# Per-layer tokens transposed and split among the last 24 down products, state rows turned in a bank of their own

## The chip, the cores and the metric

The kernel runs on one core of one Trainium2 chip. A core has five engines that run side by side: TensorE (PE in the profile; its weight loads are PEld), VectorE (DVE), ScalarE (ACT), GpSimd (POOL) and SyncE (SP). They meet through semaphores: an instruction adds to one when it ends, and another engine's queue stands still until the count is reached. Each engine works through its own queue strictly in order, so a wait holds up everything behind it on that engine. Products are written to PSUM, eight banks of 128 x 512 fp32 numbers. The metric is device time in microseconds.

## What is computed

One inference step of a two-layer encoder on 1024 prompt tokens and 64 sample tokens. Each layer is attention, a gated feed-forward part with a short convolution (ConvFFN), and a gated per-layer embedding. The change lies at the joint of the last two:

```python
def conv_ffn(h, w_in, conv_w, conv_b, w_out, pad):
    u = h @ w_in
    up = jnp.concatenate([pad, u], axis=1)
    c = conv_b + sum(up[:, j:j + T] * conv_w[j] for j in range(3))
    g, val = jnp.split(c, 2, axis=-1)
    y = (jax.nn.silu(g) * val) @ w_out
    return y, up[:, -2:]            # the state rows

def ple(x, p, g_norm, w_gate, w_proj):
    gate = jax.nn.sigmoid(rmsnorm(x, g_norm) @ w_gate)
    return (p @ w_proj) * gate      # p: 256 numbers per token and layer

x = x + conv_ffn(rmsnorm(x, ffn_norm[i]), ...)
x = x + ple(x, p[i], ...)
```

All numbers are fp32. The model's width is 1024, the feed-forward part's 2816.

## The kernel before

The residual `x` lies in SBUF with the 1024 channels in eight planes of 128 partitions and the 1088 tokens along the free dimension. Tokens are worked on in three segments (`SEGS`) of 384, 384 and 320. Every product is made from three: both operands are split into a high part (rounded) and a low part (the rest), and high x high, high x low and low x high are added up in PSUM; the three matmuls are lines L1164 to L1166. Weights come in chunks of 1024 columns; SyncE loads a chunk, ScalarE or GpSimd rounds it, and GpSimd makes the low part (L899 the rounding, L905 the rest).

**The down products.** The product with `w_out` is made in six steps `down(j)` of 24 jobs each, a job being one plane of `x` and one segment. Steps 0 to 4 take four tiles of the hidden width, the last (j = 5) only two, with six matmuls per job. A job writes one PSUM bank; VectorE adds it to `x` and counts `add_done`. In the last step the banks are `LAST_BANKS` (7, 4, 6, 5, 3), so banks 0, 1 and 2 stand free once the step before has been added. VectorE's `add_rows` (adds on L2405) also adds up planes of squares for the next norm (`squares_between`, L2415), the squares being made by ScalarE (`square`, L1782; the last plane per segment in `square_last`, L1793).

**Behind the last job**, in this order:

- TensorE turns the convolution's state rows (`tail`, two transposes on L1630) into banks 0 and 1; VectorE copies them out (L2839), ScalarE issues their stores (L2216).
- TensorE waits for the loaded per-layer tokens (`ptok`), for the copies of the state rows and for all adds, and makes 18 transposes (L1643) into banks 0 to 5.
- ScalarE rounds the six results (L2220), VectorE makes the six low parts (L2845), counted by `p_low`.
- TensorE waits for all six, and makes the norm's mean (`norm`, L1212 and L1213). ScalarE loads its table (L1799) and makes the reciprocal root (`root`, L1804, L1806), and VectorE normalises; meanwhile TensorE runs the 24 jobs of `p @ w_proj` (`row_jobs`), which ScalarE copies out between its other steps (`pj`).

The tokens are loaded by ScalarE's queue (L2208, 1 MB, and L2209, 64 KB) at the start of its `ple`. Ahead of them in that queue stands the rounding of the last weight chunk of the feed-forward part (`weights_high`, L1819), which waits until all chunks of steps 0 to 4 have been used.

Of the kernel before, what the change touches and what calls it, by code (L numbers as in the profile page):

```python
# [19 lines left out]
F32 = mybir.dt.float32  # L20
F32R = mybir.dt.float32r
ALU = mybir.AluOpType
ACT = mybir.ActivationFunctionType
AX = mybir.AxisListType

P = 128
D = 1024
KT = D // P
# [21 lines left out]
F_ADDS = 6  # L50
# [165 lines left out]
def program(nc, x_prompt, x_sample, p_prompt, p_sample, cache_a_k, cache_a_v, cache_b_k, cache_b_v,  # L216
# [6 lines left out]
    with ctx:  # L223
# [937 lines left out]
        def _(pe):  # L1161
# [357 lines left out]
            def ffn(l):  # L1519
# [67 lines left out]
                def down(j):  # L1587

                    b, tiles, wide = j % 2, 4 if j < 5 else 2, 2 if j < 5 else 4
                    for job in range(24):  # L1590
# [28 lines left out]
                        m.then_inc(gemm_done if r < 3 * wide - 1 else chunk_done, 1)  # L1619

# [7 lines left out]
                pe.wait_ge(u_kept, U_KEPT * (l + 1))  # L1628
                for kind in range(2):
                    pe.transpose(ps[0:88, kind, 0:P], tail[:, 88 * kind:88 * kind + 88], ident[:, :]).then_inc(tail_turned, 1)  # L1630

            def ple(l):
                c0 = at[f"P{l}"][0]
                nn = 2 if l == 0 else 5
                pe.wait_ge(p_loaded, 32 * (l + 1))
                pe.wait_ge(tail_kept, 2 * (l + 1))
                pe.wait_ge(add_done, ADDS[f"F{l}"] + 24 * F_ADDS)
                for k in range(2):
                    for s in range(3):
                        j = 3 * k + s  # L1640
                        for b in range(3):
                            rows = P if 3 * s + b < 8 else TS
                            m = pe.transpose(ps[:, j, 128 * b:128 * b + rows], ptok[0:rows, 3 * s + b, 128 * k:128 * k + 128],  # L1643
                                             ident[0:rows, 0:rows])
                        m.then_inc(p_turned, 1)
# [123 lines left out]
        def _(act):  # L1769
# [25 lines left out]
            def root(n, s):  # L1795

                a, w = SEGS[s]
                if s == 0:
                    act.preload_act_table_set("natural_log_exp_and_others")  # L1799
# [404 lines left out]
            def ple(l, n):  # L2204
                c0, g0 = at[f"P{l}"]
                act.wait_ge(chunk_done, c0 - 2)
# [3 lines left out]
                squares(n, add_done, ADDS[f"F{l}"] + 24 * (F_ADDS - 1), 3)  # L2210
                act.wait_ge(add_done, ADDS[f"F{l}"] + 24 * F_ADDS)
                for s in range(3):
                    square_last(n, s)
                for r, dram in enumerate((conv_p, conv_s)):
                    act.wait_ge(tail_kept, 2 * l + r + 1)
                    act.dma_start(dram[l, 0].rearrange("r (n p) -> (r n) p", p=P), tail_rows[:, r, :]).then_inc(conv_stored, 16)  # L2216
                for k in range(2):
                    for s, (a, w) in enumerate(SEGS):
                        act.wait_ge(p_turned, 6 * l + 3 * k + s + 1)
                        act.activation(act_hi[:, k, a:a + w], ps[:, 3 * k + s, 0:w], ACT.Copy).then_inc(p_high, 1)  # L2220
                act.wait_ge(conv_stored, 32 * (l + 1))
                for s in range(3):
                    root(n, s)
                for j in range(24):
# [5 lines left out]
                    a, w = SEGS[j % 3]  # L2230
# [822 lines left out]
```

## Time and profile before

| | |
|---|---|
| median of 3 runs | 3120.36 us (3115.38 to 3126.84) |
| the profiled execution | 3117.31 us, its span 3115.5 us |
| TensorE busy | 2965.0 us, 95% of the span |
| weight loads | 2858.6 us |
| VectorE busy | 2089.9 us, 67% |
| ScalarE busy | 1327.9 us, 43% |
| GpSimd busy | 1528.1 us, 49% |
| DMA | 234.23 MB, mean 75 GB/s |

The profile follows one execution on the chip. A timeline row gives the start in microseconds from the start of the span, the duration, the engine, the line of the kernel, the operation with output and input, and how often it stands in a row; brackets at the end hold the idle time before it and what ended it. An engine's name with a q (ACTq) is its queue issuing a DMA. The chain of waits is followed back from the last instruction of the program, at each step to what released it. PEclk is the clock that TensorE was granted: 1.00 is 2.4 GHz, 0.50 is 1.2 GHz.

### The profile page before, as it was taken

The page shows a single profiled execution, that of the slowest core. Times are in us where ns is not written, and L with a number is a line of the kernel's source. Part 1 is how long each engine was busy: PE and PEld are TensorE (multiplying, and loading weights), DVE is VectorE, ACT ScalarE, POOL GpSimd, SP SyncE. Part 2 cuts the span into 40 slices and gives each one's busy share as a digit, 9 for nine tenths or more (in the row PEclk, how much of TensorE's full clock was granted, in tenths as well). Part 3 has the DMA queues.
Part 4 walks back from the last instruction along what each step waited for, and adds up shares of the span by engine and source line. Part 5 has one row for each costly group of instructions (what it writes and reads, how often), then busy time and mean ns, then how long its engine had stood idle before and what let it go on. Part 6 is the DMA issues. An engine that isn't in the chain of part 4 may idle for free.

```text
span 3115.5 us, 47514 instructions
## 1 busy us (share of the span) xinstructions
PE 2965.0 (95%) x18469; PEld 2858.6 (92%) x18469; DVE 2089.9 (67%) x3171; ACT 1327.9 (43%) x2692; POOL 1528.1 (49%) x975
## 2 busy tenths in 40 slices
PE   7999999898999999999989999999899999999998
PEld 6888888798999999999978888889899999999997
DVE  6666666528888888334676777772888888833475
ACT  4555555315444443112432666651544444311243
POOL 2222122234788884212335778763488888421231
PEclk8999999899999999999989999999999999999999
DMA  5232222411222224211105121131122222421111
GB/s 118 61 72 71 75 64 69 135 42 48 77 76 79 71 77 165 98 62 57 41 15 148 31 61 53 55 129 41 55 73 74 79 70 79 162 103 58 58 39 64
DMA packets 282190, 234.23 MB, mean 75 GB/s; under 512 B 29860, under 2 KB 264052, under 8 KB 281972
## 3 DMA queue, kind: packets, MB, share of 16 engines
q1 hardware_dynamic: 267160, 217.29, 23.4%
q10 hardware_dynamic: 14812, 13.97, 1.4%
q8 instruction: 145, 2.38, 0.3%
q14 instruction: 73, 0.60, 0.1%
HBM read 168.63 MB, written 62.58 MB: 74 GB/s over the span
## 4 chain that ended last, share of the span: by engine, by line
PE 76%; DVE 14%; ACT 5%; issue 3%; POOL 1%; DMA 1%; ACTq 0%; SPq 0%; DVEq 0%; POOLq 0%
PE ps L1164 22%; PE ps L1166 21%; PE ps L1165 21%; PE ps L1347 2%; PE ps L1482 2%; ACT t L1932 2%; PE ps L1300 2%; PE ps L1283 2%; DVE t L2452 2%; PE ps L1367 2%; DVE t L2431 2%; DVE t L2602 1%; DVE t L2525 1%; ACT t L1988 1%; DVE ps L2517 1%
## 5 line engine op out<-in xcount | busy, mean ns | idle before, releaser
L1164 PE MATMUL ps<-t,t 128*128 128x384 f32 (+1 forms) x4760 | 1591.0, 334 | 48.6 <-ACT t L2106 10.4
L1166 PE MATMUL ps<-t,t 128*128 128x384 f32 (+1 forms) x4760 | 1560.9, 328 | 0.0
L1165 PE MATMUL ps<-t,t 128*128 128x384 f32 (+1 forms) x4760 | 1559.7, 328 | 0.0
L1164 PEld LDWEIGHTS ps<-t,t 128*128 128x128 f32 x4760 | 898.9, 189 | 80.3 <-issue 33.7
L1165 PEld LDWEIGHTS ps<-t,t 128*128 128x128 f32 x4760 | 900.1, 189 | 1.2 <-issue 0.5
L1166 PEld LDWEIGHTS ps<-t,t 128*128 128x128 f32 x4760 | 899.3, 189 | 0.0
L947 POOL TENSOR_TENSOR t<-t,t 128x512 fp32r<-128x512 f32 x280 | 473.6, 1710 | 31.8 <-ACT t L2057 22.1
L905 POOL TENSOR_TENSOR t<-t,t 128x1024 fp32r<-128x1024 f32 x101 | 250.4, 2479 | 435.0 <-ACT t L1819 431.6
L2802 DVE TENSOR_TENSOR t<-t,ps 128x384 f32<-128x384 f32 (+1 forms) x240 | 126.2, 531 | 274.0 <-PE ps L1166 274.0
L2731 DVE SCALAR_TENSOR_TENSOR t<-t,t,t 128x1090 f32<-128x1090 f32 x88 | 192.9, 2192 | 91.4 <-ACT t L2053 90.3
L2057 ACT ACTIVATE t<-t 128x512 fp32r<-128x512 f32 x320 | 193.1, 625 | 130.6 <-POOL t L955 50.8
L899 POOL TENSOR_TENSOR t<-t,t 128x1024 fp32r<-128x1024 f32 x51 | 104.1, 2040 | 262.1 <-PE ps L1166 261.6
L1819 ACT ACTIVATE t<-t 128x1024 fp32r<-128x1024 f32 x50 | 53.0, 1060 | 374.1 <-PE ps L1166 374.1
L1117 POOL TENSOR_TENSOR t<-t,t 128x128 f32<-128x128 f32 (+5 forms) x144 | 162.2, 1147 | 100.0 <-DVE t L2969 98.4
L2053 ACT ACTIVATE t<-t,t 128x1090 f32<-128x1090 f32 x88 | 114.7, 1304 | 224.4 <-DVE t L2716 224.4
L2733 DVE SCALAR_TENSOR_TENSOR t<-t,t,t 128x1090 f32<-128x1090 f32 x88 | 190.0, 2159 | 3.1
L2602 DVE TENSOR_TENSOR t<-ps,t 128x512 fp32r<-128x512 f32 (+1 forms) x184 | 115.6, 632 | 68.6 <-ACT t L1988 66.1
L1932 ACT ACTIVATE t<-ps,t 128x128 f32<-128x128 f32 (+5 forms) x144 | 105.6, 737 | 92.6 <-DVE t L2525 92.6
L1988 ACT ACTIVATE t<-ps 128x512 fp32r<-128x512 f32 (+1 forms) x184 | 101.2, 550 | 94.3 <-PE ps L1283 90.9
L1015 POOL TENSOR_TENSOR t<-t,t 128x384 fp32r<-128x384 f32 (+1 forms) x24 | 23.2, 966 | 225.5 <-ACT t L1956 225.5
L1482 PE MATMUL ps<-t,t 128*128 128x256 f32 (+1 forms) x656 | 118.9, 298 | 13.9 <-DVE t L2628 6.3
L955 POOL TENSOR_TENSOR t<-t,t 128x512 f32<-128x512 f32 x40 | 79.4, 1984 | 91.8 <-DMA t<-in_w_ffn_in 48.0
(191 smaller groups left out, 4071.1 us busy)
## 6 DMA issues: line engine op xcount, KB each, us to landing
t<-in_w_ffn_in SPq DMA_DIRECT2D x160, 256.0 KB, 2.9
ff_dram<-t SPq DMA_DIRECT2D x44, 544.0 KB
t<-ff_dram SPq DMA_DIRECT2D x44, 544.0 KB, 6.1
t<-in_w_ffn_out SPq DMA_DIRECT2D x44, 512.0 KB, 3.4
t<-in_w_qkv_a SPq DMA_DIRECT2D x24, 512.0 KB, 4.0
t<-in_w_ple_gate SPq DMA_DIRECT2D x16, 512.0 KB, 3.8
out<-t SPq DMA_DIRECT2D x32, 192.0 KB, 2.1
t<-in_w_o_a SPq DMA_DIRECT2D x8, 512.0 KB, 4.1
```

The costliest lines, as they stand in the source:

```text
L905: pool.tensor_tensor(w_lo[slot][:, :], w_raw[slot][:, :], w_hi[slot][:, :].bitcast(F32), ALU.subtract).then_inc(w_split, 1)
L947: pool.tensor_tensor(lo, raw, hi.bitcast(F32), ALU.subtract).then_inc(blk_split, 1)
L1117: pool.tensor_tensor(probs, probs, rz[:, c + m:c + m + 1].broadcast_to([P, w]), ALU.mult).then_inc(scaled, 1)
L1164: pe.matmul(out, a_hi, b_hi, start=start, stop=False, skip_group_check=True)
L1165: pe.matmul(out, a_hi, b_lo, start=False, stop=False, skip_group_check=True)
L1166: return pe.matmul(out, a_lo, b_hi, start=False, stop=stop, skip_group_check=True)
L1482: mm = pe.matmul(ps[:, 6, 0:256], v_both[r:P, vi, :], part[r:P, k % 2, 256 * b:256 * b + 256], start=g == 0 and b == 0 and part is bT_hi, ...
L1932: act.activation(p_a[n % 2][:, m, 0:w], psf[:, 1024 * m:1024 * m + w], ACT.Exp, bias=negmax[:, col:col + 1], accum_out=zsum[:, col:col + 1 ...
L2057: act.activation(S[name][0], S[name][2], ACT.Copy).then_inc(blk_high, 1)
L2602: dve.tensor_tensor(bT_lo[:, k % 2, 0:w], ps[:, 4 + k % 2, 0:w], bT_hi[:, k % 2, 0:w].bitcast(F32), ALU.subtract).then_inc(t_free, 1)
L2731: dve.scalar_tensor_tensor(dst, ub[:, 1:T + 3], col(44), dst, ALU.mult, ALU.add).then_inc(conv_step, 1)
L2733: dve.scalar_tensor_tensor(dst, ub[:, 0:T + 2], col(0), dst, ALU.mult, ALU.add).then_inc(conv_step, 1)
```

## The change

The 18 transposes of the per-layer tokens move from behind the last 24 down jobs to among them: nine behind job 1 and nine behind job 7, both into banks 0 to 2. ScalarE rounds each group between its squares, VectorE makes the low parts behind its adds 4 and 10. The state rows are turned into one bank, 3, at two offsets. ScalarE loads the table of the root before it waits for the last adds, issues the stores of the state rows behind the roots, and waits for these stores only before it copies out job 12 of `p @ w_proj`. The wait for chunks ahead of the token loads goes out.

```diff
--- before.py
+++ after.py
@@ -1617,6 +1617,22 @@
                             m = three(ps[:, bank, 0:w], w_hi[c % 2][:, cc:cc + 128], w_lo[c % 2][:, cc:cc + 128],
                                       h_hi[:, 4 * b + k, a:a + w], h_lo[:, 4 * b + k, a:a + w], k == 0, k == tiles - 1)
                         m.then_inc(gemm_done if r < 3 * wide - 1 else chunk_done, 1)
+                        if j == 5 and job in (1, 7):
+                            turn_layer_tokens(job // 6)
+
+                def turn_layer_tokens(k):
+
+                    if k == 0:
+                        pe.wait_ge(p_loaded, 32 * (l + 1))
+                        pe.wait_ge(add_done, a0 + 112 + JOB_BANKS.index(0) + 1)
+                    else:
+                        pe.wait_ge(p_low, 6 * l + 3)
+                    for s in range(3):
+                        for b in range(3):
+                            rows = P if 3 * s + b < 8 else TS
+                            m = pe.transpose(ps[:, s, 128 * b:128 * b + rows], ptok[0:rows, 3 * s + b, 128 * k:128 * k + 128],
+                                             ident[0:rows, 0:rows])
+                        m.then_inc(p_turned, 1)
 
                 first_up(c0)
                 for n in range(PAIRS):
@@ -1626,23 +1642,15 @@
 
                 pe.wait_ge(tail_set, 2 * NU * (l + 1))
                 pe.wait_ge(u_kept, U_KEPT * (l + 1))
+                pe.wait_ge(add_done, a0 + 24 * F_ADDS - 4)
                 for kind in range(2):
-                    pe.transpose(ps[0:88, kind, 0:P], tail[:, 88 * kind:88 * kind + 88], ident[:, :]).then_inc(tail_turned, 1)
+                    pe.transpose(ps[0:88, 3, 128 * kind:128 * kind + 128], tail[:, 88 * kind:88 * kind + 88],
+                                 ident[:, :]).then_inc(tail_turned, 1)
 
             def ple(l):
                 c0 = at[f"P{l}"][0]
                 nn = 2 if l == 0 else 5
-                pe.wait_ge(p_loaded, 32 * (l + 1))
-                pe.wait_ge(tail_kept, 2 * (l + 1))
                 pe.wait_ge(add_done, ADDS[f"F{l}"] + 24 * F_ADDS)
-                for k in range(2):
-                    for s in range(3):
-                        j = 3 * k + s
-                        for b in range(3):
-                            rows = P if 3 * s + b < 8 else TS
-                            m = pe.transpose(ps[:, j, 128 * b:128 * b + rows], ptok[0:rows, 3 * s + b, 128 * k:128 * k + 128],
-                                             ident[0:rows, 0:rows])
-                        m.then_inc(p_turned, 1)
                 pe.wait_ge(p_low, 6 * (l + 1))
                 norm(nn)
                 row_jobs(c0, 0, 0, act_hi, act_lo, pj_kept, lambda k: 24 * l + k)
@@ -1792,10 +1800,10 @@
                 act.wait_ge(acc_done, 6 * (n - 1) + 5)
                 act.activation(sq[1][:, a:a + w], x[:, KT - 1, a:a + w], ACT.Square).then_inc(sq_last, 1)
 
-            def root(n, s):
+            def root(n, s, loaded=False):
 
                 a, w = SEGS[s]
-                if s == 0:
+                if s == 0 and not loaded:
                     act.preload_act_table_set("natural_log_exp_and_others")
                 if n:
                     act.wait_ge(mean_done, 3 * (n - 1) + s + 1)
@@ -2203,24 +2211,30 @@
 
             def ple(l, n):
                 c0, g0 = at[f"P{l}"]
-                act.wait_ge(chunk_done, c0 - 2)
                 act.wait_ge(ff_low, NFF * (l + 1))
                 act.dma_start(ptok[:, 0:8, :], p_prompt[l, 0].rearrange("(b p) d -> p b d", p=P)).then_inc(p_loaded, 16)
                 act.dma_start(ptok[0:TS, 8, :], p_sample[l, 0]).then_inc(p_loaded, 16)
-                squares(n, add_done, ADDS[f"F{l}"] + 24 * (F_ADDS - 1), 3)
+
+                def layer_tokens_high(k):
+
+                    for s, (a, w) in enumerate(SEGS):
+                        act.wait_ge(p_turned, 6 * l + 3 * k + s + 1)
+                        act.activation(act_hi[:, k, a:a + w], ps[:, s, 0:w], ACT.Copy).then_inc(p_high, 1)
+
+                for k in range(KT - 1):
+                    if k in (1, 3):
+                        layer_tokens_high(k // 2)
+                    act.wait_ge(add_done, ADDS[f"F{l}"] + 24 * (F_ADDS - 1) + 3 * (k + 1))
+                    square(n, k)
+                act.preload_act_table_set("natural_log_exp_and_others")
                 act.wait_ge(add_done, ADDS[f"F{l}"] + 24 * F_ADDS)
                 for s in range(3):
                     square_last(n, s)
+                for s in range(3):
+                    root(n, s, True)
                 for r, dram in enumerate((conv_p, conv_s)):
                     act.wait_ge(tail_kept, 2 * l + r + 1)
                     act.dma_start(dram[l, 0].rearrange("r (n p) -> (r n) p", p=P), tail_rows[:, r, :]).then_inc(conv_stored, 16)
-                for k in range(2):
-                    for s, (a, w) in enumerate(SEGS):
-                        act.wait_ge(p_turned, 6 * l + 3 * k + s + 1)
-                        act.activation(act_hi[:, k, a:a + w], ps[:, 3 * k + s, 0:w], ACT.Copy).then_inc(p_high, 1)
-                act.wait_ge(conv_stored, 32 * (l + 1))
-                for s in range(3):
-                    root(n, s)
                 for j in range(24):
                     half = j // 12
                     if j % 12 < 11:
@@ -2228,6 +2242,8 @@
                     else:
                         act.wait_ge(chunk_done, c0 + half + 1)
                     a, w = SEGS[j % 3]
+                    if j == 12:
+                        act.wait_ge(conv_stored, 32 * (l + 1))
                     act.activation(pj[:, j // 3, a:a + w], ps[:, 4 + j % 4, 0:w], ACT.Copy).then_inc(pj_kept, 1)
                     high_step(n, j)
 
@@ -2833,17 +2849,27 @@
                 add_tiles(0, range(4, 24))
                 for j in range(1, 5):
                     add_tiles(j)
-                add_rows(c0 + 24, g0 + 108, 0, 0, 0, squares_between(2 + 3 * l, 22), LAST_BANKS)
+
+                def layer_tokens_low(k):
+
+                    for s, (a, w) in enumerate(SEGS):
+                        dve.wait_ge(p_high, 6 * l + 3 * k + s + 1)
+                        dve.tensor_tensor(act_lo[:, k, a:a + w], ps[:, s, 0:w], act_hi[:, k, a:a + w].bitcast(F32),
+                                          ALU.subtract).then_inc(p_low, 1)
+
+                add_squared = squares_between(2 + 3 * l, 22)
+
+                def between(job):
+                    add_squared(job)
+                    if job in (4, 10):
+                        layer_tokens_low(job // 6)
+
+                add_rows(c0 + 24, g0 + 108, 0, 0, 0, between, LAST_BANKS)
+                dve.wait_ge(tail_turned, 2 * l + 2)
                 for kind in range(2):
-                    dve.wait_ge(tail_turned, 2 * l + kind + 1)
-                    dve.tensor_copy(tail_rows[:, kind, :], ps[0:88, kind, 0:P]).then_inc(tail_kept, 1)
+                    dve.tensor_copy(tail_rows[:, kind, :], ps[0:88, 3, 128 * kind:128 * kind + 128]).then_inc(tail_kept, 1)
             def ple(l, n):
                 c0, g0 = at[f"P{l}"]
-                for k in range(2):
-                    for s, (a, w) in enumerate(SEGS):
-                        dve.wait_ge(p_high, 6 * l + 3 * k + s + 1)
-                        dve.tensor_tensor(act_lo[:, k, a:a + w], ps[:, 3 * k + s, 0:w],
-                                          act_hi[:, k, a:a + w].bitcast(F32), ALU.subtract).then_inc(p_low, 1)
                 normalise(n)
                 dve.wait_ge(pj_kept, 24 * (l + 1))
                 st = n
```

## Rows read from the trace of the kernel before

**Rows 1.** Page of the profile, chain that ended last: shares by engine.

```profile
PE 76%; DVE 14%; ACT 5%; issue 3%; POOL 1%; DMA 1%; ACTq 0%; SPq 0%; DVEq 0%; POOLq 0%
```

**Rows 2.** Timeline of TensorE, first of the last 24 products: start, us, instruction.

```profile
1449.93 0.34 PE L1164 MATMUL ps<-t,t 128*128 128x384 f32 x1
...
1452.04 0.31 PE L1164 MATMUL ps<-t,t 128*128 128x320 f32 x1
...
1452.91 0.34 PE L1164 MATMUL ps<-t,t 128*128 128x384 f32 x1
```

**Rows 3.** Timeline of ScalarE, same stretch, with its DMA issues.

```profile
1450.27 0.37 ACTq L2208 DMA_DIRECT2D t<-in_p_prompt  x1
1450.68 0.61 ACTq L2209 DMA_DIRECT2D t<-in_p_sample  x1
```

**Rows 4.** Chain of waits, end of layer 0's down products: start, us, what.

```profile
1470.91 1.29 DVE t L2415
...
1472.63 1.12 ACT t L1782
1473.78 1.29 DVE t L2415
...
1475.51 0.52 ACT t L1793
...
1476.81 0.39 ACT t L2220
1477.22 2.76 DVE t L2845 x6
1480.02 0.91 PE ps L1212 x2
1480.93 0.65 PE ps L1213 x2
```

**Rows 5.** Timeline of TensorE, behind layer 0's down products.

```profile
1475.97 2.50 PE L1643 MATMUL ps<-t,t 128*128 128x128 f32 x18 [1.82 <-DVE t L2839]
```

**Rows 6.** Lines L2208, L2209 (issue to landing) and L2216 (ns of an issue).

```profile
DMA to landing us min/median/max: 5.4/5.4/5.4
...
DMA to landing us min/median/max: 5.5/5.6/5.7
...
L2216 ACTq DMA_DIRECT2D out<-t x4: 325/348/580, 1475.7 to 2954.6; - x4
```

**Rows 7.** Timelines of ScalarE and TensorE, the same place in layer 1.

```profile
2929.24 0.62 ACTq L2209 DMA_DIRECT2D t<-in_p_sample  x1
...
2930.59 0.31 PE L1164 MATMUL ps<-t,t 128*128 128x320 f32 x1
```

**Rows 8.** Timelines of GpSimd and VectorE, weight passes beside vector work.

```profile
1474.02 2.81 POOL L899 TENSOR_TENSOR t<-t,t 128x1024 fp32r<-128x1024 f32 x1 [5.83 <-PE ps L1166]
...
1498.41 2.60 POOL L905 TENSOR_TENSOR t<-t,t 128x1024 fp32r<-128x1024 f32 x1
...
1498.67 2.75 DVE L2431 TENSOR_TENSOR t<-t,t 128x384 fp32r<-128x384 f32 x1
```

**Rows 9.** Windows: length, busy PE, PEld, DVE, ACT, POOL, PEclk, DMA share.

```profile
754.00:759.00 5.00, 0.72 (x5) 0.46 (x4) 4.96 (x4) 0.00 (x0) 2.55 (x3) 1.00 0.37 123
...
760.00:762.00 2.00, 2.00 (x7) 2.00 (x8) 1.58 (x4) 2.00 (x5) 1.23 (x1) 0.50 0.01 4
...
763.00:765.00 2.00, 2.00 (x14) 2.00 (x13) 1.97 (x2) 1.51 (x3) 1.29 (x1) 1.00 0.00 0
...
1476.00:1478.50 2.50, 2.46 (x18) 1.92 (x18) 1.28 (x3) 2.50 (x8) 2.42 (x2) 1.00 0.14 36
...
1612.80:1623.00 10.20, 7.64 (x19) 5.66 (x19) 7.46 (x10) 8.39 (x12) 3.12 (x2) 0.50 0.00 0
```

**Rows 10.** Timeline of TensorE, the next norm's mean; idle before it in brackets.

```profile
1602.62 1.65 PE L1212 MATMUL ps<-t,t 128*128 128x384 f32 x2 [2.16 <-DVE t L2415]
1604.06 1.49 PE L1213 MATMUL ps<-t,t 128*128 128x384 f32 x2
```

## Prediction, made before the changed kernel was run

> **What bounds the kernel now.** I first read the page's chain of work that ended last: the matrix engine holds three quarters of it and the vector engine a seventh [rows 1]. A change of a few microseconds has to be judged in its own stretch, so I then read the timelines around the last 24 down products and the start of the per-layer embedding, once per layer.
>
> In the last 24 products TensorE runs without a break: one group of three jobs starts at 1449.93 and the next at 1452.91, so three jobs take 2.98 us, two wide and one narrow [rows 2]. Behind the products the chain of waits leaves TensorE [rows 4]. VectorE adds a plane of squares, then the last product; ScalarE squares the last plane (1475.51), rounds the transposed tokens (1476.81), VectorE makes their low halves (six in 2.76 us), and only then does the mean of the norm start, at 1480.02. TensorE's only work in that hole is the tail's two transposes and the eighteen token transposes, 2.50 us [rows 5]. From the start of the last square to the mean 4.51 us pass per layer; that is all the change can win.
>
> ScalarE issues the two token loads at 1450.27 and 1450.68 [rows 3], a third of a microsecond and more into the first of these 24 jobs. They land 5.4 and 5.5 to 5.7 us after issue [rows 6]. Before the change nobody needs them until 1475.97, so this lateness costs nothing. The new code moves the user to where the lateness shows.
>
> **The change part by part**, both layers together unless it says otherwise.
>
> *Removed from the chain (A).* The mean no longer waits for the roundings, the low halves and the transposes; it waits for the last product's sum and one square (0.52 us) [rows 4]. The table load moves ahead of that wait, where ScalarE has nothing else to do; it was hidden behind the low halves before. With a hand-over of some 0.03 us the mean starts 0.55 us after 1475.51 in place of 4.51. A = 2 x (0.55 - 4.51) = -7.9.
>
> *Added wait for the tokens (B).* The first nine transposes stand behind job 1 and wait for both loads. Job 1's last product has been issued by 1452.04 [rows 2]. The deleted wait for chunks on ScalarE wins no time: the same count is waited for by the weight rounding just ahead (`weights_high` of the last chunk), so the loads cannot be issued earlier. They are complete at 1450.68 + 5.7 = 1456.38; TensorE stands 4.34 us. In layer 1: 2929.24 + 5.5 = 2934.74 against 2930.59 [rows 7], 4.15 us. All products behind stand in order on TensorE, and so do the adds and squares that follow them. B = +8.5, between 7.2 (if the larger load alone counted, 3.63 us per layer) and 9.5 (half a microsecond of hand-over each). The other new wait there, for the add of the job that last used bank 0, is over long before: that job ended in the group before.
>
> *Transposes inside the products (C).* Eighteen at 2.50 us per layer [rows 5], now in a stream that TensorE sets: +5.0. They were on the chain before too; that part is already in A.
>
> *The second turn* waits for three low halves. Counted from the end of the first turn: job 2's sum, ScalarE's first square 1.12 us, three roundings at 0.39, three low halves at 0.46 [rows 4] put the third low half about 5.1 us later; six jobs take 2 x 2.98 = 5.96. It is hidden with 0.8 us to spare, at most 1.4 us per layer (three low halves) if not: taken as 0.
>
> *VectorE falls behind (D).* The three low halves of the second turn (1.4 us) stand behind add 10; some 0.3 us of it fits into VectorE's idle time, so 1.1 us of lag remain. Afterwards a plane of squares is added once per three jobs, each behind a square that waits for an add. Two such sums in the lagging state start at 1470.91 and 1473.78, 2.87 us apart [rows 4], against 2.98 us of three jobs [rows 2]: the lag shrinks by only 0.1 us a period, and some 0.8 us is left at the last add, three periods on. Beyond that, the last sum of squares now meets GpSimd. Before, it starts at 1473.78 and GpSimd's weight pass at 1474.02 [rows 4, 8]: VectorE is first by 0.24 us. With 0.8 us of lag it comes second, and where it comes second an operation on two SBUF operands takes 2.75 us while the weight pass runs [rows 8]; a low half of the same shape from PSUM takes 0.46 [rows 4]. I take half of about 1.4 us for this. D = 2 x (0.8 + 0.7) = +3.0, from 0 to 2 x (1.4 + 2.3) = 7.4.
>
> The Trainium skill (GPSIMD Engine Reference, section 8, Key points) has GpSimd share its SBUF interfaces with VectorE, against instructions with two SBUF inputs. By that rule the token low halves, which read PSUM, would run on undisturbed and the sums of squares would not; with the last sum blocked in full D would be 2 x (0.8 + 2.3) = +6.2 and the total below 17.4.
>
> *The clock behind the stall (E).* An idle of about five microseconds from 754.7 on is followed by 0.50 of the clock, that is 1.2 GHz, in 760 to 762, and by the full level after 763 [rows 9]. Some 3 us of products at half speed lose 1.5 us. I expect the same behind B: E = 2 x 1.5 = +3.0, from 0 to 3.4.
>
> *The clock at the mean (F).* In the old hole the eighteen transposes stand in the middle and the clock stays at 1.00 [rows 9]. Now the hole is one idle of 2.5 to 4 us. After one of 2.16 us the two pairs of the next norm's mean run from 1602.62 to 1605.55, 2.93 us [rows 10], against 0.91 + 0.65 = 1.56 here [rows 4]: 1.37 us per layer. I take 1.0: F = +2.0, from 0 to 3.4.
>
> The Trainium skill (TensorE: Matmul & The Clock Gate, Part 4: PE-mode transpose) says the full clock does not engage for transposes. By it the old hole should already have dropped, and moving the transposes would cost nothing, with F at 0 and the total at 12.2; the row shows 1.00 through the hole, and I go by the row.
>
> *Moved stores (G).* ScalarE now issues the two state stores between the roots and the first product copy. An issue takes 0.35 us in the median, at most 0.58 [rows 6]; the product copies have four banks in hand, so only the first normalised tile feels it. G = +0.6, from 0 to 1.8. The wait for these stores stands before copy 12 of 24, long after they have landed. The tail's transposes wait for add 19, which is done four jobs before; free.
>
> Sum: -7.9 + 8.5 + 5.0 + 3.0 + 3.0 + 2.0 + 0.6 = +14.2. The profiled execution took 3117.31, so 3131.5; the median of the runs is 3.05 higher, which gives 3134.6. I say 3133, +0.4%, just inside the half per cent (15.6 us) that a measurement of this kernel can about tell from no change.
>
> **The rivals.**
>
> *The tokens are there in time.* Then B and E vanish: 14.2 - 8.5 - 3.0 = +2.7, 3120.0 to 3123.1, and with D and F at their lower ends 7.9 - 5.0 - 0.6 = 2.3 us faster, 3115. It decides if the loads land within 1.4 us of the second issue. For it: a wait in ScalarE's queue ahead of the loads goes out. Against it: the landing of 5.4 to 5.7 us in both layers, and the issue still behind the same count. Chance 0.08.
>
> *The half clock lasts.* From 1612.8 to 1623.0 the clock stays at 0.50, with TensorE in short waits [rows 9]. If the products behind the stall run like that for 10 us, E is 2 x 5 = 10: total +21.2, 3138.5 to 3141.6, slower by 0.7%. It decides as soon as the half level lasts some 1.4 us longer per layer than my 3 us. For it: short waits do follow, for the second turn and the banks. Against it: behind the closest case in kind, a wait and then dense products, it lasted 3 us. Chance 0.10.
>
> *VectorE loses every meeting with GpSimd.* D = 7.4 in place of 3.0: +18.6, 3135.9 to 3139.0, slower by 0.6%. For it: the lead today is only 0.24 us. Against it: sums of squares in the middle of the stretch got through before. Chance 0.17.
>
> **How the numbers follow.** My forecast, stall with a sum of 8 to 18, has 0.65; of it about a fifth lies above 15.6. The lower ends give -7.9 + 7.2 + 5.0 = +4.3, the upper ends 22 to 23. So the range runs from 3119 to 3143. Slower by over 0.5%: 0.13 of my forecast, 0.10 and most of 0.17, 0.37. Faster by over 0.5% would need more than A itself: 0.02. The rest, 0.61, is within.
>
> **What would show it.** TensorE idle of 4 us behind job 1 of the last 24, ended by the token load; a granted clock of 0.50 for some 3 us behind it; the last product's sum of each layer some 8 to 10 us later than now, and the mean some 0.55 us after the last square begins. I am wrong if the load's landing is not what TensorE waits for, if the clock stays at 1.00 after the stall (then the total is nearer 9), or if the mean waits for something else, such as a table load at the roots.

## The result, and the profile after

The changed kernel takes 3137.66 us in the median of 4 runs (3137.37 to 3141.03), the kernel before, beside it, 3120.85 (3115.38 to 3126.84): ratio 1.0055, interval 1.0038 to 1.0072. On the medians it is 16.8 us slower; 3133 was forecast. The profiled execution took 3141.03 us, with a span of 3139.2. One execution of the wait-only kernel below took 4249.8 us at a granted clock of 0.63 and is left out of its median.

The timeline of TensorE of the changed kernel, layer 0 (start, length, line; idle before it in brackets), answers to [rows 2, 5]. L1633 are the token turns, L1647 the tail's turn, L1212 and L1213 the mean, L1164 a product.

```profile
1456.95 2.26 PE L1633 MATMUL ps<-t,t 128*128 128x128 f32 x9 [4.06 <-DMA t<-in_p_sample]
...
1459.14 0.63 PE L1164 MATMUL ps<-t,t 128*128 128x320 f32 x1
...
1466.70 1.24 PE L1633 MATMUL ps<-t,t 128*128 128x128 f32 x9
...
1483.76 0.38 PE L1647 MATMUL ps<-t,t 128*88 128x128 f32 x2
...
1488.14 1.62 PE L1212 MATMUL ps<-t,t 128*128 128x384 f32 x2 [4.00 <-ACT t L1801]
1489.55 1.49 PE L1213 MATMUL ps<-t,t 128*128 128x384 f32 x2
...
1494.14 0.58 PE L1164 MATMUL ps<-t,t 128*128 128x384 f32 x1
```

There are two holes of 4 us, one ended by the load of the sample's tokens, one by the last square. Behind each everything is slow: nine transposes take 2.26 us, while the second nine, with no wait, take 1.24. The windows of the same kernel (start:end, length, busy time of PE, PEld, DVE, ACT, POOL, granted clock, DMA share, GB/s) give the reason; they answer to [rows 9].

```profile
1455.00:1456.00 1.00, 0.00 (x0) 0.00 (x0) 0.00 (x0) 0.00 (x0) 0.00 (x0) 0.83 0.86 264
1456.00:1457.00 1.00, 0.05 (x1) 0.05 (x1) 0.00 (x0) 0.00 (x0) 0.00 (x0) 0.50 0.91 329
...
1461.00:1462.00 1.00, 1.00 (x5) 1.00 (x4) 0.49 (x1) 0.34 (x1) 0.00 (x0) 0.50 0.00 0
1462.00:1463.00 1.00, 1.00 (x6) 1.00 (x5) 0.12 (x1) 1.00 (x2) 0.00 (x0) 0.76 0.00 0
...
1487.00:1488.00 1.00, 0.00 (x0) 0.00 (x0) 0.84 (x4) 0.53 (x2) 1.00 (x1) 0.50 0.00 0
...
1492.00:1493.00 1.00, 1.00 (x3) 0.58 (x2) 0.75 (x2) 0.21 (x1) 0.00 (x0) 0.50 0.51 153
```

The clock falls to 0.50 (1.2 GHz) inside the stall and is back in 1462 to 1463: some 6.8 us at the half level. TensorE works in 5.5 of them, where the prediction had 3. At the mean the half level is as long, with TensorE working in 5.1 of it. The last view is the chain of waits of the changed kernel (it answers to [rows 4]) and, below it, GpSimd's timeline ([rows 8]).

```profile
1472.91 1.26 DVE t L2857 x3
...
1475.82 2.48 DVE t L2431
1478.30 0.41 DVE t L2421
...
1479.88 1.29 DVE t L2431
...
1485.62 1.43 DVE t L2431
...
1487.47 0.53 ACT t L1801
1488.01 0.14 issue
1488.14 1.62 PE ps L1212 x2
```

```profile
1474.75 2.41 POOL L905 TENSOR_TENSOR t<-t,t 128x1024 fp32r<-128x1024 f32 x1
```

The mean starts 0.67 us behind the first of the last squares, where it was 4.51: the part that was meant to win did so. But from 1471 on the chain no longer goes through TensorE, whose products are done at 1483.76. It goes through VectorE and ScalarE: through the three low halves of the second turn (L2857), then through the sum of squares at 1475.82, which begins while GpSimd's pass runs and takes 2.48 us. The page's shares by engine say less:

```profile
PE 68%; DVE 19%; ACT 7%; issue 4%; POOL 1%; DMA 1%; ACTq 0%; SPq 0%; DVEq 0%; POOLq 0%
```

TensorE has eight points less than in [rows 1], some 250 us, where the joint grew by 21. Most of that shift must be the chain taking another way elsewhere in the kernel; it was not traced.

### The profile page after: what moved, and what is told of

It is laid out like the page before. It is cut to its first block, busy times and chain, and to the rows that moved or that the text cites. A ratio compares the mean times of both kernels' runs of the same rounds, so it can differ in the third digit from the quotient of the medians.

```text
span 3139.2 us, 47516 instructions
## 1 busy us (share of the span) xinstructions
PE 2978.8 (95%) x18469; PEld 2870.0 (91%) x18469; DVE 2090.9 (67%) x3171; ACT 1329.3 (42%) x2692; POOL 1510.7 (48%) x975
## 4 chain that ended last, share of the span: by engine, by line
PE 68%; DVE 19%; ACT 7%; issue 4%; POOL 1%; DMA 1%; ACTq 0%; SPq 0%; DVEq 0%; POOLq 0%
PE ps L1164 19%; PE ps L1166 18%; PE ps L1165 18%; PE ps L1347 2%; DVE t L2747 2%; PE ps L1482 2%; ACT t L1940 2%; DVE t L2749 2%; PE ps L1300 2%; PE ps L1283 2%; PE ps L1367 2%; DVE t L2447 1%; DVE t L2468 1%; ACT t L2061 1%; DVE t L2618 1%
## 5 line engine op out<-in xcount | busy, mean ns | idle before, releaser
L1164 PE MATMUL ps<-t,t 128*128 128x384 f32 (+1 forms) x4760 | 1594.4, 335 | 49.5 <-ACT t L2114 10.4
L1164 PEld LDWEIGHTS ps<-t,t 128*128 128x128 f32 x4760 | 901.3, 189 | 80.5 <-issue 34.5
L947 POOL TENSOR_TENSOR t<-t,t 128x512 fp32r<-128x512 f32 x280 | 462.8, 1670 | 34.4 <-ACT t L2065 23.5
```

The costliest lines, as they stand in the source:

```text
L947: pool.tensor_tensor(lo, raw, hi.bitcast(F32), ALU.subtract).then_inc(blk_split, 1)
L1164: pe.matmul(out, a_hi, b_hi, start=start, stop=False, skip_group_check=True)
```

## The experiments

Each kernel below was timed beside the kernel before on the same chip. The table gives, for the profiled execution of each, the path through the joint in three pieces (layer 0 / layer 1, us): from the first of the last 24 products to the tail's turn; from there to the mean; from there to the first per-layer product copy on ScalarE. "Joint" is the sum over both layers less that of the kernel before (70.2); "median" is the difference of the medians.

```
kernel           to tail's turn  to mean      to first copy  joint   median  ratio [95%]
before           23.84 / 23.84   6.25 / 6.24  5.02 / 5.03
changed          33.15 / 33.51   4.38 / 4.38  8.00 / 8.00    +21.2   +16.8   1.0055 [1.0038, 1.0072]
changed, again   32.09 / 33.17   4.38 / 4.39  7.19 / 7.81    +18.8   +16.8   1.0061 [1.0048, 1.0075]
wait only        29.49 / 29.66   6.38 / 6.41  7.08 / 7.06    +15.9   +15.0   1.0043 [1.0029, 1.0057]
early load       26.43 / 26.41   4.38 / 4.38  7.20 / 8.21     +6.8    +5.9   1.0016 [1.0006, 1.0026]
turns in hole    32.08 / 33.87   4.38 / 4.39  5.50 / 5.28    +15.3   +18.1   1.0054 [1.0041, 1.0067]
early turns      26.42 / 26.41   2.40 / 2.40  7.19 / 6.97     +1.6    +2.2   1.0006 [0.9996, 1.0016]
early, filled    26.42 / 26.43   2.40 / 2.40  5.49 / 5.28     -1.8    -3.3   0.9990 [0.9981, 0.9999]
rows in hole     26.42 / 26.43   2.41 / 2.40  5.49 / 5.28     -1.8    -1.3   1.0000 [0.9991, 1.0009]
GpSimd later     26.40 / 26.40   3.07 / 3.06  5.49 / 5.35     -0.4    +4.4   1.0014 [1.0005, 1.0023]
stall filled     30.59 / 30.62   4.38 / 4.38  8.44 / 6.97    +15.2   +10.5   1.0035 [1.0023, 1.0047]
second in hole   25.14 / 25.14   2.41 / 2.40  5.49 / 5.28     -4.4    -5.0   0.9982 [0.9973, 0.9991]
stores later     25.14 / 25.15   2.39 / 2.40  4.98 / 4.98     -5.2    -1.4   0.9996 [0.9987, 1.0005]
products first   34.17 / 33.31   4.39 / 4.38  7.19 / 8.20    +21.4   +18.3   1.0063 [1.0046, 1.0079]
```

Single executions of one kernel differ by 10 us and more, so the two columns agree to a few microseconds at best. The kernels were timed in several groups, each beside the kernel before; where the text gives a difference of two medians of different groups, the one by the table stands beside it.

**The wait alone.** Before, and in its last 24 products:

```
                        m.then_inc(gemm_done if r < 3 * wide - 1 else chunk_done, 1)
+                       if j == 5 and job == 1:
+                           pe.wait_ge(p_loaded, 32 * (l + 1))
```

> The kernel before, with one line more: behind job 1 of the last 24 down products TensorE waits for the token loads of the layer. Nothing is moved; the transposes stay behind the products. Theory (the stall and the half clock behind it are what costs): TensorE stands about 4.1 us per layer behind job 1 and the six jobs behind it run some 2.7 us longer, so 2 x (4.1 + 2.7) = 13.6 us over the kernel before, about 3134. Rival (the stall is absorbed, since VectorE and ScalarE set the end of the stretch; what costs is the transposes and what stands behind them): 0 to 3 us over the kernel before, 3121 to 3124.

Measured +15.0: the wait by itself costs nearly as much as the whole change, with not one transpose moved. That the two are so close is partly chance, since this kernel has neither the change's gain (A of the prediction) nor its losses C, D and G. Its timeline of TensorE:

```profile
1455.13 0.63 PE L1164 MATMUL ps<-t,t 128*128 128x320 f32 x1 [3.95 <-DMA t<-in_p_sample]
...
1480.60 3.13 PE L1645 MATMUL ps<-t,t 128*128 128x128 f32 x18 [1.81 <-DVE t L2841]
1484.78 1.65 PE L1212 MATMUL ps<-t,t 128*128 128x384 f32 x2 [1.05 <-DVE t L2847]
```

The stretch is 5.65 us longer, 3.95 of it the wait, 1.70 the half clock behind it; in layer 1 5.82, 4.12 and 1.70. The rest lies at the mean: the hole there is as before, with the eighteen transposes in it, and yet the clock falls, at 1482.2, in the middle of the transposes (3.13 us for what took 2.50 [rows 5], first copy 2 us later). Why it does here and not before, the runs don't tell. The expectation had 6.8 us per layer in the stretch and nothing at the mean, so its sum of 13.6 fits better than its parts.

**The loads earlier.** The changed kernel with the two token loads, and the wait ahead of them, moved before the last `weights_high` of the down chunks (issued at 1438.77 and 1439.18 in place of 1450.89 and 1451.30).

> The changed kernel, with the two token loads of each layer issued by ScalarE ahead of the rounding of the last chunk's weights, some 12 us earlier. Theory: no wait behind job 1 and no half clock behind it, so about 13.4 us less than the changed kernel, near 3124, with the hole at the mean and its half clock still there (mean to first normalised job about 6 us). Rival (TensorE finds the next limit at once, such as VectorE's queue, or the transposes themselves are the cost): at most 5 us less, 3133 or more.

Measured +5.9 over before, 11 us less than the changed kernel. The first turn then has no wait and takes 1.24 us; the stretch is 26.43, that is 23.84 and 2.59 for eighteen transposes.

**The changed kernel again**, and **the hole at the mean filled**:

```
+                pe.wait_ge(p_low, 6 * (l + 1))
+                for _ in range(24):
+                    pe.transpose(ps[:, 1, 0:P], ident[:, :], ident[:, :])
                 pe.wait_ge(add_done, ADDS[f"F{l}"] + 24 * F_ADDS)
-                pe.wait_ge(p_low, 6 * (l + 1))
                 norm(nn)
```

> The changed kernel once more, unaltered, as the measure for what stands beside it. Both theories: its median lies 16 to 18 us over the kernel before (3136 to 3138). A rival for the fill of the hole alone: if it lies more than 3 us above 3137.2, the filled hole had gained as much, and its lack of effect was the spread of few runs.

> The changed kernel, with 24 transposes of the identity (their result is used by nobody) in the hole of about 4 us ahead of the mean, behind the wait for the last token low half. Theory (the idle at the mean is what drops the clock, and transposes hold it): the clock stays near 1.00 through the hole and behind it, mean to first normalised job about 3.5 us in place of 6.1, so about 5 us less than the changed kernel, near 3133; the wait behind job 1 stays. Rival (transposes do not count for the clock): the granted clock falls to 0.50 at the mean as in the changed kernel, no difference, or up to 2 us more.

The changed kernel repeats its result (3137.29). Filling the hole does to the mean what the theory said, 2.5 and 2.7 us against the changed kernel's first profile, but the median is 3137.19: nothing gained. In the two profiles 1.8 us of the 5.9 gained at the joint are lost again by the end of the kernel. In the windows of the filled kernel the next norm's mean, behind its idle of 2.16 us, falls to half clock:

```profile
1611.00:1613.00 2.00, 2.00 (x6) 1.40 (x6) 0.06 (x1) 0.73 (x3) 0.00 (x0) 0.50 0.00 0
```

and in those of the changed kernel the same place does not, as it did before [rows 10]:

```profile
1613.00:1615.00 2.00, 1.32 (x5) 0.87 (x5) 1.65 (x3) 1.64 (x2) 0.00 (x0) 1.00 0.00 0
```

That is 1.6 us. Why the medians show nothing at all stays open. The changed kernel's first profile is a long execution; in its second, the half clock at the mean of layer 0 lasted 3.4 us in place of 6.8, and against that one the joint's gain is only 3.5 us.

**Turns and low halves earlier.** Early loads; turns behind jobs 0 and 4, low halves behind sums 1 and 5. And **GpSimd later**: early loads alone, with GpSimd held until the last sum:

```
-                        if j == 5 and job in (1, 7):
-                            turn_layer_tokens(job // 6)
+                        if j == 5 and job in (0, 4):
+                            turn_layer_tokens(job // 4)
...
+            pool.wait_ge(add_done, ADDS["F0"] + 24 * F_ADDS)
             splits(f0 + f_chunks, ck)
```

> The early token loads, and besides them the two turns of the tokens moved forward, behind jobs 0 and 4 in place of 1 and 7, with the roundings ahead of the first and second square and the low halves behind sums 1 and 5, so that VectorE has caught up before it adds the first plane of squares. Theory (VectorE's lag comes from the low halves of the second turn, which push a sum of squares behind GpSimd's weight pass): tail turn to last sum about 1.2 us in place of 3.2, so about 4 us less than with the early loads alone, near 3120. Rival (where the low halves stand makes no difference; the lag is the transposes' and the squares' own): within 1 us of the early loads alone.

> Early token loads only, and GpSimd begins the weight passes of the per-layer chunks only when the last down product has been added, so that none of them runs beside the sums of squares. Prediction's theory (part of VectorE's lag is a sum of squares held up by GpSimd's pass, part is the low halves): that sum takes 1.28 us in place of 2.48, tail turn to last sum 2.0 us in place of 3.2, so 2.4 us less than with early loads alone, near 3122.6. Rival (the lag comes from the low halves in VectorE's order alone): tail turn to last sum stays at 3.2 us. A third outcome, worse: the passes come too late for the per-layer products, and TensorE waits for weights behind the mean.

With the turns early the mean comes 1.98 us sooner per layer and the median is 3.7 lower: the lag is one of order in VectorE's queue, and another order removes it at no cost. The second kernel divides it. VectorE's timeline with early loads alone, then with GpSimd held back (the same sum of squares):

```profile
1468.56 2.48 DVE L2432 TENSOR_TENSOR t<-t,t 128x1088 f32<-128x1088 f32 x1 [0.25 <-ACT t L1790]
```

```profile
1466.81 1.29 DVE L2434 TENSOR_TENSOR t<-t,t 128x1088 f32<-128x1088 f32 x1 [0.26 <-ACT t L1792]
```

Tail's turn to last sum is 3.21 us, 1.88 and, with early turns, 1.21: of 2.0 us of lag 1.33 is GpSimd's and 0.67 the low halves'. Held back, GpSimd's passes collide with the start of the norm instead. VectorE's first two operations there take 3.80 us together (1.15 in the changed kernel), the next 2.76 where its like take 0.55:

```profile
1480.54 3.80 DVE L2471 SCALAR_TENSOR_TENSOR t<-t,t,t 128x384 f32<-128x384 f32 x2 [3.04 <-ACT t L1816]
1484.26 2.76 DVE L2450 TENSOR_TENSOR t<-t,t 128x384 fp32r<-128x384 f32 x1
```

Later TensorE waits 1.17 and 1.90 us for product copies, where with early loads alone it waits once, 1.53 (layer 0), and in each layer the clock falls to 0.50 for 6.8 us there. So that kernel ends 0.1 us from the early loads (1.5 under them by the table), though its joint is 7.2 us shorter.

**The hole filled, with the rest mended.** On the kernel with early turns: 16 transposes nobody uses; or the first two per-layer products; or the second turn itself, which then leaves the products and goes into banks 4 to 6, each behind the sum that frees it. The last two kernels use the banks of the down products in the order 4, 5, 6, 7, 3. Core of the last one's edit:

```
                                  ident[:, :]).then_inc(tail_turned, 1)
+                turn_layer_tokens(1)
...
-                pe.wait_ge(p_low, 6 * (l + 1))
                 norm(nn)
+                pe.wait_ge(p_low, 6 * (l + 1))
```

> Early token loads and early turns, and besides them 16 transposes of the identity (used by nobody) in the hole of 2.02 us ahead of the mean. Theory (an idle of 2 us ahead of the mean drops the clock, transposes hold it, and what that saves is kept to the end): mean to first row job 3.5 us in place of 5.18, so 3.3 us less than with early loads and turns alone, near 3118. Rival (the saving is given back, because the clock falls at a later wait instead): the mean is as fast, but the time within 1 us of early loads and turns alone.

> Early token loads and early turns, and besides them real work in the hole: the first two of the 24 per-layer products of tokens run ahead of the mean (the last 24 down products use their banks in the order 4, 5, 6, 7, 3, so that banks 4 and 5 are free by then). Theory: the clock stays full at the mean, and two products of about 1.04 us each are gone from behind it, 2 x (1.66 + 2.08) = 7.5 us less than with early loads and turns alone, near 3114, about 5 us under the kernel before. Rival (the norm's own work on VectorE and ScalarE sets the end of the per-layer products, so that TensorE being early changes nothing, or the clock falls at a later wait instead): within 2 us of early loads and turns alone.

> Early token loads, first turn of the tokens behind job 0, and the second turn (nine transposes, 1.24 us) taken out of the products and put behind the tail's turn, in the hole ahead of the mean, into banks 4 to 6; its roundings stand around the last squares on ScalarE and its low halves behind the tail's copies on VectorE, and only the first row job waits for them. Theory: 1.24 us per layer leave the stream that TensorE sets, and the transposes hold the clock at the mean (1.66 us per layer), so 2 x 2.9 = 5.8 us less than with both turns early (3121.3), near 3115.5, about 5 us under the kernel before. Rival (1.24 us of work in a hole of 2 us doesn't hold the clock): 2.5 us less, near 3119. Other rival (the roundings push the roots back, or the next stage on VectorE takes the gain): 3121 or more.

Here the fill is kept: 4.1 us less than the early turns (5.5 by the table). Of TensorE's timeline, first of the early turns, then filled:

```profile
1478.87 1.40 PE L1212 MATMUL ps<-t,t 128*128 128x384 f32 x2 [2.02 <-ACT t L1801]
```

```profile
1473.92 1.91 PE L1655 MATMUL ps<-t 128*128 128x128 f32 x16
1476.10 0.88 PE L1212 MATMUL ps<-t,t 128*128 128x384 f32 x2 [0.27 <-ACT t L1803]
```

The empty hole alone does not settle whether the clock falls. The profiles here have fourteen holes of 2.0 to 4.0 us ahead of the mean that stayed empty, and at twelve of them the clock fell; they have ten that were filled, and it fell at none. The two exceptions are those of 2.68 us with GpSimd held back: the clock stayed at 1.00.

Two real products in the hole bring less than transposes do: 3.5 us less than the early turns by the table, where 7.5 were expected. Their joint is as good, with 2.1 us of products already done. Behind it VectorE is held up by GpSimd's next pass, which starts at 1492.85 (VectorE's timeline):

```profile
1493.48 2.25 DVE L2477 SCALAR_TENSOR_TENSOR t<-t,t,t 128x384 f32<-128x384 f32 x1
1495.65 2.72 DVE L2456 TENSOR_TENSOR t<-t,t 128x384 fp32r<-128x384 f32 x1
```

The same two operations are held up in the other kernels as well (2.27 and 2.75 us in the kernel before, 2.25 and 2.76 with the 16 transposes), so this is not what sets the products apart. What differs is TensorE, two products ahead: it waits twice for a product copy, where with the 16 transposes it waits once, 1.51 us. In the second wait, or just behind it, the clock falls, for 6.8 us in layer 0 and 3.4 in layer 1. Its timeline, and a window behind the second wait:

```profile
1496.66 0.44 PE L1164 MATMUL ps<-t,t 128*128 128x384 f32 x1 [0.92 <-ACT t L2256]
...
1499.89 0.69 PE L1164 MATMUL ps<-t,t 128*128 128x384 f32 x1 [1.90 <-ACT t L2256]
```

```profile
1500.00:1502.00 2.00, 2.00 (x7) 2.00 (x8) 2.00 (x5) 1.75 (x5) 0.00 (x0) 0.50 0.69 207
```

The second turn in the hole is the best version, 5.0 us under the kernel before. Besides the 16 transposes, whose interval ends at 0.9999, it is the only one whose interval lies below 1. Its timeline of TensorE:

```profile
1473.37 1.24 PE L1632 MATMUL ps<-t,t 128*128 128x128 f32 x9
1475.56 0.88 PE L1212 MATMUL ps<-t,t 128*128 128x384 f32 x2 [0.95 <-ACT t L1801]
```

**The stores later.** The same, with the two state stores issued behind the third product copy.

> The same with the second turn in the hole, and ScalarE issues the two state stores behind the third of the per-layer product copies in place of ahead of the first. Theory (the stores' issue of 0.95 us stands ahead of the first normalised tile and costs about 0.5 us per layer): 1 us less than without this, near 3114.5. Rival (those 0.5 us are covered by the product copies' banks): no difference within 0.5 us.

The first copy comes 0.51 and 0.30 us earlier, then ScalarE stands 1.21 us for the same two issues between copies. TensorE's wait for a product copy near the end of the per-layer products grows from 1.52 to 1.88 us, and behind it this kernel is 0.5 us late. The issue costs its time wherever it stands. In layer 1 the same wait of 1.88 us, in place of 1.31, is followed by half clock (window below), and the per-layer products end 2.2 us later than without this edit, counted from the first of the 24 down products. That is over half of the 4.0 us between the two profiled executions; the medians differ by 3.6.

```profile
2980.00:2982.00 2.00, 2.00 (x8) 2.00 (x7) 2.00 (x5) 1.87 (x5) 0.00 (x0) 0.50 0.00 1
```

**The stall filled.** The changed kernel, late loads and all, with 34 unused transposes ahead of the wait for them.

> The changed kernel (late token loads), with 34 transposes of the identity (used by nobody, about 3.9 us of work) between job 1 of the last 24 products and the wait for the tokens: the stall stays as long, but TensorE is busy in it. Theory (what the half clock behind the stall costs is a term of its own, 2.5 to 2.9 us per layer, caused by the idle): the clock stays at 1.00 behind the wait, the nine transposes take 1.24 us in place of 2.26, and the time is 5 us less than the changed kernel's 3137.3, near 3132. Rival (the saving is given back at later waits, or transposes don't hold the clock for so long): within 1.5 us of the changed kernel.

> The changed kernel (late token loads, the wait behind job 1 as it is), with the first turn of the tokens moved behind job 4 and the second behind job 10, so that products and not transposes stand first behind the stall; the low halves move with them, behind sums 7 and 13. Theory (the half clock behind a stall lasts longer where transposes stand first: 1.7 us lost with products first, 2.6 with the nine transposes): granted clock of 0.50 for about 3.4 us behind the stall in place of 6.6, nine transposes in 1.24 us, and TensorE's stretch up to the tail's turn shorter by 0.9 us or more per layer; in all 2 us less than the changed kernel's 3137.3, less what VectorE loses because the second turn's low halves stand nearer to the end. Rival (the order makes no difference, the stall's length alone sets how long the half clock lasts): 6 us or more at 0.50, and the stretch up to the tail's turn as long as in the changed kernel.

Filled, it takes 7.1 us less than the changed kernel (6.3 by the table), though the tokens come no sooner. TensorE's timeline:

```profile
1450.29 3.87 PE L1628 MATMUL ps<-t 128*128 128x128 f32 x34
1454.42 1.30 PE L1635 MATMUL ps<-t,t 128*128 128x128 f32 x9 [0.25 <-DMA t<-in_p_sample]
```

The last run asked why the half clock lasted 3.4 us in the wait-only kernel and 6.8 in the changed one: products or transposes first behind the stall. The theory fell. With products first, windows of layer 0 and of layer 1:

```profile
1452.00:1453.00 1.00, 0.00 (x0) 0.00 (x0) 0.00 (x0) 0.00 (x0) 0.00 (x0) 0.50 0.82 239
...
1457.00:1458.00 1.00, 1.00 (x5) 1.00 (x5) 0.49 (x1) 0.00 (x0) 0.00 (x0) 0.50 0.00 0
```

```profile
2943.00:2944.00 1.00, 0.85 (x3) 0.85 (x4) 0.00 (x0) 0.00 (x0) 0.00 (x0) 0.53 0.81 315
...
2946.00:2947.00 1.00, 1.00 (x6) 1.00 (x5) 0.12 (x1) 0.79 (x1) 0.00 (x0) 0.77 0.00 0
```

One kernel shows both lengths, 6.8 us and 3.4, behind stalls of 3.89 and 3.87 us. So does the changed kernel on its second profile (3.4 us in layer 0, 6.8 in layer 1), and so does the kernel with 24 transposes at the mean, whose stall is as in the changed kernel (3.4 and 6.8). In ten such stalls of four kernels, five are long and five short. Four of the long ones are those where the clock fell 0.5 to 1.6 us before the stall ended; in the short ones it fell from 0.3 us before to 0.5 us behind its end. The fifth long one does not fit: there the clock fell 0.23 us before the end, where two short ones have 0.25 and 0.27. What decides when the clock falls and for how long is open. Moved so late, the second turn also makes TensorE wait for low halves (0.20 us) and a bank (0.55), so the whole is no faster.

## Why the prediction was right, and what in it was off

The direction, the bound and the place were right: the median lies in the range, 4.7 us over the forecast. The ratio, 1.0055, is just over the half per cent that had been given 0.37, against 0.61 for staying within; the interval covers both. Term by term, both layers, predicted and then measured in the changed kernel's profile:

- **A, what leaves the chain**: -7.9, and -7.7 (0.67 against 4.51 twice). The table load, 1.28 us, was hidden.
- **B, the stall for the tokens**: +8.5, and 4.06 + 4.05 = +8.1. Shown twice over, by the wait alone and by the early loads. The rival that the tokens are there in time is out.
- **C, eighteen transposes in the stream**: +5.0, and 2 x 2.59 = +5.2.
- **D, VectorE's lag**: +3.0, and 2 x 1.99 = +4.0. Right in kind: the low halves leave 0.67 us (0.8 was said), a meeting with GpSimd costs 1.33 (0.7, half of one, was said). But the sum that loses is one in the middle of the stretch, not the last, which took 1.43 us. The rival that VectorE loses every meeting is out: of the six sums of squares this one alone lost over a microsecond. The argument against it was too strong, though: in the kernel before, too, one sum in the middle of the stretch began inside a pass and took 1.73 us.
- **E, the half clock behind the stall**: +3.0. This step was mis-sized. It was taken as 3 us at half speed from [rows 9]; the stretch to the tail's turn less that of the early loads and less the stall gives 33.15 - 26.43 - 4.06 = 2.66 and 33.51 - 26.41 - 4.05 = 3.05, +5.7, outside the 0 to 3.4 that was given. The short form costs 1.7 per layer, about what the sum had (1.5); five of the ten stalls are long ones.
- **F, the half clock at the mean**: +2.0. Mis-sized in the same way: first row job 6.00 and 6.21 us behind the mean's start in place of 3.52, +5.2, again outside its 0 to 3.4. Of this not all reaches the end, as the filled hole showed.
- **G, the stores**: +0.6; the first copy moves by 2.98 us in layer 0 and 2.97 in layer 1, where the first row job moves by 2.48 and 2.69: +0.5 and +0.3, +0.8.
- **The second turn** was free, as said: no wait at 1466.70.

The measured terms sum to 21.3, the joint in the table to 21.2, the medians to 16.8. The joint has the same number as the rival in which the half clock lasts (+21.2), but by chance: E was 5.7 and not 10, F 5.2 and not 2.0. The 4.4 us between joint and medians lie within the spread of single executions. The two that were profiled differ by 23.7 us, so nothing of the joint's 21.2 is given back in them; the changed one lies 3.4 us over its median, the one before 3.5 under. The changed kernel's second profile has +18.8 at the joint and 15.8 in the span, with 2.3 us less than the kernel before already ahead of the joint. So the nearness of the forecast to the medians is in part luck: its sum of 14.2 is 2.6 short of the medians, but 7.1 short of the measured terms, most of it E and F.

Of the signs that were named, the idle of 4 us, its end by the token load and the mean's wait came as said. The half level was longer, and the last product's sum came 11.3 us later in layer 0, counted from the first of the 24 products, where 8 to 10 were said.

Transposes held the clock in the fills: with 34 of them in the stall and 16 in the hole it stayed at 1.00 in both layers, and what stood behind them ran at full speed. They do not always: in the wait-only kernel it fell during eighteen of them, behind an idle of 1.81 us. The Trainium skill (TensorE: Matmul & The Clock Gate, Part 4: PE-mode transpose) says the full clock does not engage for transposes; the fills disagree, as [rows 9] did. By that rule neither fill could have changed the time.

A sum of squares that began inside GpSimd's pass took 2.48 us against 1.29, and sums from PSUM beside it 0.47 to 0.55. The Trainium skill (GPSIMD Engine Reference, section 8, Key points) names instructions with two SBUF inputs as those that contend; the trace agrees.

## What to carry to other kernels

A consumer moved forward needs its load moved forward too: here 11 of the 17 us lost came from a load issued in time for the old place and 5 us late for the new one. A stall of TensorE has to be priced with the half clock behind it, here 1.7 to 3 us for one of 4 us, and work put into a hole can be worth more than the same work taken out of it: the second turn, back in the hole, is the best version. Small gains then hang on the waits further on and on whether the clock falls there, as the two early products and the later stores showed.

## What the hardware showed that was not expected

- Behind like stalls of 3.9 to 4.3 us the half clock lasted either some 3.4 us or some 6.8, within one kernel.
- Transposes of an identity, used by nobody, made a kernel 7.1 us faster in the stall (3137.3 to 3130.2) and 4.1 us faster in the hole (3121.3 to 3117.2); by the table 6.3 and 5.5. In the hole of the changed kernel, with its stall left as it was, they gained nothing.
- An operation of VectorE on two SBUF operands that starts while GpSimd's pass runs took 2.25 to 2.76 us in place of 0.55 to 0.61. A pair of them stands in the per-layer products of the kernel before as well.
- An idle of 2.02 us ahead of the mean was followed by half clock in both layers, one of 2.68 us in another kernel in neither.
